# Turning the experts' silu rows by identity products instead of transposes, in a mixture-of-experts and attention kernel

## The reference, cut to what matters

```python
def expert_block(args):
    idx, e = args
    xb = x_pad[idx]
    hb = jax.nn.silu(xb @ w_gate[e]) * (xb @ w_up[e])
    return hb @ w_down[e]
```

## Time and profile before

| what | value |
|---|---|
| median of 3 runs | 1968.73 us (1968.09 to 1969.48) |
| span of the profiled execution | 1967.0 us |
| TensorE busy | 1906.8 us, 97% of the span |
| VectorE busy | 796.4 us, 40% |
| ScalarE busy | 432.2 us, 22% |
| bytes moved | 512.32 MB, 260 GB/s over the span |

### The profile page before, as it was taken

How to read it: one execution, slowest core, us unless ns; L and a number is a source line. 1 busy time by engine, 2 the same in 40 slices (tenths; PEclk the granted TensorE clock), 3 DMA queues, 4 the chain that set the end, 5 groups by cost and what they waited for, 6 DMA issues and landing times.

```text
span 1967.0 us, 22022 instructions
## 1 busy us (share of the span) xinstructions
PE 1906.8 (97%) x8622; PEld 995.8 (51%) x8622; DVE 796.4 (40%) x2049; ACT 432.2 (22%) x885; POOL 88.5 (4%) x116
## 2 busy tenths in 40 slices
PE   8999999999999899999999999999989999999999
PEld 5886644444444335544464444444433474564565
DVE  4653354221121143445535422112114438886663
ACT  2000111111111024166311101111102532224553
POOL 0000000000000010023000000000002000000000
PEclk9999999999999999999999999999989999999999
DMA  7825399999999992221449999999999331220000
GB/s 305 197 80 224 142 393 409 429 427 427 428 428 428 423 360 93 81 86 43 195 165 394 402 426 428 428 428 429 427 419 339 148 123 43 86 86 1 12 12 22
DMA packets 49558, 512.32 MB, mean 260 GB/s; under 512 B 5408, under 2 KB 7584, under 8 KB 19488
## 3 DMA queue, kind: packets, MB, share of 16 engines
q1 hardware_dynamic: 40992, 480.86, 60.1%
q0 software_dynamic: 8448, 29.89, 4.0%
HBM read 484.38 MB, written 26.35 MB: 260 GB/s over the span
## 4 chain that ended last, share of the span: by engine, by line
PE 86%; DMA 6%; DVE 3%; ACT 2%; issue 2%; POOL 1%; SPq 0%; DVEq 0%; POOLq 0%; ACTq 0%
PE ps L1126 21%; PE ps L1170 10%; PE ps L1093 8%; PE ps L534 6%; PE ps L1992 6%; PE ps L745 5%; PE ps L1541 5%; DMA ring<-in_wexp 4%; PE ps L1709 3%; PE ps L2324 3%; PE ps L1740 2%; PE ps L2364 2%; PE ps L2181 1%; PE ps L1195 1%; PE ps L2345 1%
## 5 line engine op out<-in xcount | busy, mean ns | idle before, releaser
L1126 PE MATMUL ps<-ring,arena 128*48 128x512 f32 x1504 | 387.6, 602 | 29.7 <-DMA ring<-in_wexp 15.5
L1126 PEld LDWEIGHTS ps<-ring,arena 128*48 128x48 f32 x1504 | 115.0, 124 | 222.6 <-issue 221.2
L1139 DVE TENSOR_TENSOR arena<-arena,ps 48x512 f32<-48x512 f32 x64 | 44.2, 690 | 440.6 <-ACT arena L1133 440.5
L1093 PEld LDWEIGHTS ps<-arena,h 128*128 128x128 f32 x1024 | 158.8, 190 | 46.2 <-issue 46.2
L1170 PE MATMUL ps<-ring,arena 128*48 128x512 f32 x768 | 173.6, 592 | 3.5 <-DMA ring<-in_wexp 2.4
L1093 PE MATMUL ps<-arena,h 128*128 128x192 f32 (+1 forms) x1024 | 174.8, 325 | 0.0
L1126 PE MATMUL ps<-arena 128*48 128x512 f32 x544 | 169.6, 594 | 0.6 <-issue 0.6
L1133 ACT ACTIVATE arena<-ps 48x512 f32<-48x512 f32 x64 | 37.8, 591 | 458.6 <-PE ps L1126 458.6
L1992 PE MATMUL ps<-ring,arena 128*128 128x512 f32 (+3 forms) x384 | 132.7, 500 | 0.8 <-DVE arena L372 0.8
L1541 PE MATMUL ps<-ring,arena 128*128 128x512 f32 x256 | 112.3, 593 | 1.3 <-DMA ring<-in_wall 0.7
L745 PE MATMUL ps<-ring,arena 128*128 128x512 f32 x256 | 112.8, 594 | 0.1
(11 more groups left out here) (311 smaller groups left out, 2290.0 us busy)
## 6 DMA issues: line engine op xcount, KB each, us to landing
ring<-in_wexp SPq DMA_DIRECT2D x136, 2048.0 KB, 20.5
arena<-in_wexp SPq DMA_DIRECT2D x50, 2048.0 KB, 17.4
ring<-in_wall SPq DMA_DIRECT2D x25, 2048.0 KB, 7.6
ring<-in_wexp SPq DMA_DIRECT2D x12, 1024.0 KB, 14.2
y_d<-arena POOLq DMA_DIRECT2D x60, 192.0 KB, 7.1
yo_d<-gbuf SPq DMA_DIRECT2D x2, 4032.0 KB, 46.3
ring<-in_wall SPq DMA_DIRECT2D x3, 1536.0 KB, 9.2
xs_d<-h POOLq DMA_DIRECT2D x8, 512.0 KB, 7.5
```

What stands on the lines that cost most here:

```text
L1093: mm = pe.matmul(banks[4 + t % 2][:, k * 4 * CAP + z0:(k + 1) * 4 * CAP], h[:, i, kk * P:(kk + 1) * P], RT["sel"][:, NT * (p_ % 2) + i, z0 ...
L1126: mm = pe.matmul(outs[m], xeT[:, e_ // 4 % 2, k, e_ % 4 * CAP:(e_ % 4 + 1) * CAP], ws[m][:, k, :], start=(k == 0), stop=(k == KT - 1))
L1139: dve.tensor_tensor(hh[0:CAP, e_ % 2, :], sl[0:CAP, e_ % 2, :], banks[1][64:64 + CAP, :], ALU.mult).then_inc(S["hh"], 1)
```

## The change

`pe_ht` turns `hh` by an ordinary float32 product in place of a transpose. It reads all 128 partitions of the buffer, with the identity's first 48 columns as the moving operand. So that partitions 48 to 127 add zeros, `dve_router` sets both buffers of `hh` to zero once in each layer. The overflow blocks keep their transposes.

```diff
@@ dve_router
             st.did(dve.memset(yy[:, 0, :], 0.0))
+            st.did(dve.memset(hh, 0.0))
             st.wait()
@@ pe_ht
             for k in range(4):
-                mm = pe.transpose(banks[6][:, k * CAP:(k + 1) * CAP], hh[0:CAP, e_ % 2, k * P:(k + 1) * P], ident[0:CAP, 0:CAP])
+                mm = pe.matmul(banks[6][:, k * CAP:(k + 1) * CAP], hh[:, e_ % 2, k * P:(k + 1) * P], ident[:, 0:CAP], start=True, stop=True)
             mm.then_inc(S["ht"], 1)
```

## The result

The changed kernel takes 1973.47 us (median of 10 runs, 1971.44 to 1975.03); the kernel before, run beside it, 1968.14 us (1964.04 to 1969.93). The ratio is 1.0028, 95% interval 1.0020 to 1.0036: 5.3 us slower, where I had forecast 11.3. The way was right and the size was not: less than half of it came.

The account below looks back on a forecast made before the run. TensorE (97% busy) and full DMA queues were taken to set the pace by turns. Layer 0's 6.4, layer 1's 4.3 and last turns' 1.1, less 0.5 for the clock, gave 11.3 us on 1968.73: 1980.0 us, range 1969.5 to 1987.0.

Parts of the forecast that it names:

- Two limits side by side, the load queue absorbing the first part: Expert stages: TensorE and DMA both near full; delayed load issue moves no landing while the queue holds work.
- The turn, 0.53 us: Each expert's turn of `hh` on TensorE takes 0.53 us longer, between 0.49 and 0.58; 33.9 us for 64 turns.
- 26 turns paid in full: By expert 26 TensorE has 26 x 0.53 = 13.8 us added per layer, before subtracting weight waits and queue slack.
- The last turn, 2 x 0.53 us with nothing to cover it: Expert 31's turn, followed by each layer's last down product, is fully exposed: 1.1 us for both layers.
- Stock, 5.7 and 5.8 us: Load queue's slack at expert 26 in layers 0 and 1, from landings of 13.2 and 13.3 against 7.5 us.
- The memset: Zeroing `hh` on VectorE makes expert 0's `hh` 0.45 us late but costs nothing, with 0.08 us to spare.
- The clock, -0.5 us: Shorter waits should keep later gate and up products at 7.07 us; counted -0.5 us, bounds 0 and -2.5.
- the loads cover it all: Rival: the load queue has enough in hand everywhere, only last turns count; +1.1 us, 1969.8 us; chance 0.13.
- faster, by the clock: Rival: loads cover the turns and three slow passes return to 7.07 us; -4.4 us, 1964.3 us; chance 0.04.
- all exposed: Rival: all 64 turns' added TensorE time is paid; +33.9 us, 2002.6 us; chance 0.03.
- four loads: Rival: each turn product needs four weight loads, 1.50 us more a turn; +64 us, 2033 us; chance 0.03.

Follow-up runs that it names:

- the large dose: Kernel before with 16 extra 128x512 products (13.8 us) ahead of expert 20's turn, once a layer: ratio 1.0065, +12.8 us.
- the small dose: Kernel before with 5 extra 128x512 products (4.3 us) ahead of expert 20's turn, once a layer: ratio 0.9993, -1.4 us.
- the run with the dose at expert 31: Kernel before with 20 extra identity products ahead of expert 31's turn, once a layer, meant as 4.5 us: ratio 1.0057, +11.2 us.
- the run with it at expert 28: Kernel before with the same extra identity products ahead of expert 28's turn alone: ratio 1.0005, +1.0 us.

## Why the prediction was off

Point by point, by its own steps:

- *Two limits side by side, the load queue absorbing the first part*: held. The dip of the DMA share, the first landing at 8.2 us (layer 0; 9.5 in layer 1, so some 2 us of stock were left there), the vanished waits of experts 25 to 27, the rise from turn to turn, and no loss from a dose of 4.3 us.
- ***The turn, 0.53 us*: the first term that was mis-sized.** It is 0.45: 0.92 us to the next product for 0.37, begun 0.10 earlier, where the rows gave 0.95 at most and 0.09. I had both rows, took a middle between counting and not counting the early start, and took 0.115 us for a spacing that is 0.111 (with the products made twice, eight records more take 0.89 us more). The true value lay below my likely ends (0.49 to 0.58). 0.08 x 26 in two layers is 4.2 us.
- ***26 turns paid in full*: the second.** At experts 3, 11 and 15 an idle time of 0.43 us followed the transposes. I took a clean expert as the pattern for all. Lengthening work that stands in front of a wait is free up to the wait's length. TensorE reached expert 26 later by 384.57 - 375.75 = 8.8 us in layer 0 and 384.54 - 377.53 = 7.0 in layer 1. Of 26 x 0.45 = 11.7, the weight waits took 1.7 and 3.7; the rest that is missing, 1.2 and 1.0, went in these waits and that of expert 1. It is a net figure: they took more, and experts 0 and 7 cost 0.33 and 0.20 us more than the others, 0.14 of it the memset. One execution's waits are not sure to more than 1 us: in the run with the memset alone the wait behind expert 15 in layer 1 is 1.0 us shorter.
- ***The last turn, 2 x 0.53 us with nothing to cover it*: the third.** The down product does come 0.53 us later (1.55 us after the turn's start for 1.02), but before the change VectorE was busy with gathered rows for 0.75 us after it, and the next stage waits for VectorE. From turn 31 to that stage it is 6.25 and 6.24 us for 6.24 and 6.21: the term is nothing, and 1.1 us comes off. With half the weights loaded VectorE is done in time, and there the last turn is paid: 6.03 us for 5.49. I had followed TensorE's own order to its end, and not what the next stage waits for.
- *Stock, 5.7 and 5.8 us*: right to about 1 us a layer. From expert 26's gate product to the next stage it took 92.11 and 93.03 us before and 87.52 and 87.64 after, so 4.6 and 5.4 us were absorbed, turns 26 to 31 included. Once the queue is dry the figure stays: 87.4 to 88.1 us in the runs with the large dose and with 48 rows, which came to expert 26 as much as 13 us late.
- *The memset*: nearly held, 0.14 us a layer for nothing.
- *The clock, -0.5 us*: wrong. I read the gap ahead of expert 29 as a wait for weights, which a later TensorE would shorten. The profile names DMA as its releaser, since the last unit landed near its end; the run with half loads has the gap without any shortage. Of the three slow passes only that of expert 30 in layer 1 came back to 7.07 us; the two at expert 29 grew, to 9.89 and 9.99.

Put together with the measured numbers: 8.8 - 4.6 = 4.2 and 7.0 - 5.4 = 1.6, 5.8 us by the stages of the two traces, and 5.3 (3.9 to 7.1) by the medians. From my 11.3 to it: 4.2 by the turn, 2.2 by the waits for gathered rows and 1.1 by the last turns, less 1.5 for stock that I had put too high and 0.5 for the clock. The last two errors went the other way, so that the total came nearer to the truth than its terms: that is luck. Single executions scatter: the code ahead of layer 0's experts, unchanged, took 0.8 us less, and the span grew by 4.8.

Of the rivals, *the loads cover it all* needed a stock that was not there (landings of 8.2 and 9.5 us), *faster, by the clock* fails by the longer passes at expert 29, *all exposed* by the small dose, and *four loads* by the x8. The Trainium skill's advice (Perfetto Trace Analysis, Transposes) to use a transpose and not a standard matmul agrees with the trace: the transpose of the same padded block takes 0.53 us, the product 0.92.

## What to carry to other kernels

When work is lengthened on an engine that feeds a queue, add up the time until the queue's narrowest point, and subtract every wait that stands right behind the lengthened work on the way; look at all instances of it, not at a clean one. A releaser named for a gap is the last event before its end, not its cause: take the supposed cause away before a gain is counted on it. At the end of a stage, look at what the next stage waits for, on every engine, before the last piece of work is called exposed. A term that is multiplied by 52 needs its hundredths: here 0.08 us in it made 4.2 us of the forecast.

## What the runs showed of the hardware

- A float32 product with a 48-row stationary block was slower than the same one padded with zeros to 128 rows: 1.02 for 0.92 us for four, and begun 0.09 us later, since its first weight load did not start while the 128-row matmuls before it were in flight. The padded load did, 0.16 us ahead. The transposes show the same: with 48 rows the first load starts with its matmul, after 0.23 us of idle time, padded to 128 rows 0.16 us ahead of it (428.91 for 429.07 us). The Trainium skill (TensorE: Matmul & The Clock Gate, "The mechanism") says that weight loads overlap matmuls in flight only where their row groups differ; a sentence before that it also names loads into the background weight buffer, which no run here can tell apart. Here both blocks fill all 128 rows and the load overlapped, so the first rule by itself does not hold in this trace; the measurement decides.
- In streams of 40 records of 48-column products the granted clock fell from 1.00 to 0.50 though TensorE was never idle in them: between 707 and 708 us in the run with the dose at expert 31 (begun at 705.23, behind a wait of 1.1 us that ended at 701.66), and between 664 and 666 us in the run with it at expert 28 (begun at 660.30, with no wait since 649.86). The products behind them took 6.20 for 3.64 us and 9.41 for 7.07.
